# S5 stage of a hybrid decoder trunk: rounding of the frames' turns and the cosines on ScalarE, order and width of GpSimd's projection work

## What is computed

```python
lam = lax.complex(jnp.minimum(a_re, LAMBDA_RE_MAX), a_im)
dt = jnp.exp(log_dt)[:, None]
lam_bar = jnp.exp(lam * dt)
b_bar = ((lam_bar - 1.0) / lam)[:, :, None] * lax.complex(b_re, b_im)
bu = lax.complex(einsum('blgc,gpc->blgp', ug, real(b_bar)), einsum('blgc,gpc->blgp', ug, imag(b_bar)))
_, states = lax.associative_scan(combine, (a, bu), axis=1)   # s[t] = lam_bar*s[t-1] + bu[t]
y = einsum('blgp,gcp->blgc', real(states), c_re) - einsum('blgp,gcp->blgc', imag(states), c_im)
...
return val * jax.nn.sigmoid(gate)     # z = gelu(y + d*u) @ w_glu + b_glu
```

## Time and profile before

| what | value |
|---|---|
| median of 3 runs | 1022.61 us (1021.65 to 1023.76) |
| profiled execution, its own time | 1020.7 us |
| its span | 1018.9 us |
| TensorE busy | 997.9 us, 98% of the span |
| VectorE busy | 820.6 us, 81% |
| ScalarE busy | 487.2 us, 48% |
| GpSimd busy | 274.5 us, 27% |
| granted TensorE clock, mean | 0.994 of full speed |
| chain that ended last, by engine | PE 83%, DVE 10%, issue 3%, ACT 2%, POOL 1% |

### The profile page before, as it was taken

The page is one execution under the profiler, slowest core; times in us unless marked ns, Lnnn a source line. Parts: engine busy times, 40 slices in busy tenths (PEclk is TensorE's granted clock), DMA queues, the critical chain, the costliest instruction groups (busy, mean ns, idle before and its releaser), DMA issues.

```text
span 1018.9 us, 16672 instructions
## 1 busy us (share of the span) xinstructions
PE 997.9 (98%) x5858; PEld 822.7 (81%) x5858; DVE 820.6 (81%) x1154; ACT 487.2 (48%) x883; POOL 274.5 (27%) x231
## 2 busy tenths in 40 slices
PE   9799999999999999999999999999999999999997
PEld 4687888888888888888887776888888888888886
DVE  7994588798898988986895776889898898989844
ACT  7773323444355444543422878655354354543421
POOL 8995887300000000030967240010000000001151
PEclk9899999999999999999999999999999999999998
DMA  6124334122412233230333110232322412224012
GB/s 256 35 47 131 141 107 142 64 84 90 159 62 103 103 118 109 82 124 1 104 128 119 49 42 21 87 123 102 104 84 82 151 76 103 84 102 163 22 42 83
DMA packets 31877, 97.53 MB, mean 96 GB/s; under 512 B 10696, under 2 KB 13256, under 8 KB 27984
## 3 DMA queue, kind: packets, MB, share of 16 engines
q1 hardware_dynamic: 31824, 96.83, 27.3%
HBM read 92.36 MB, written 2.10 MB: 93 GB/s over the span
## 4 chain that ended last, share of the span: by engine, by line
PE 83%; DVE 10%; issue 3%; ACT 2%; POOL 1%; DVEq 0%; ACTq 0%; POOLq 0%
PE ps L1792 17%; PE ps L1795 9%; PE ps L1813 8%; PE ps L1814 8%; PE ps L1815 8%; PE ps L1752 6%; PE ps L1753 6%; PE ps L1754 6%; PE ps L1695 2%; PE ps L1697 2%; PE ps L1696 2%; DVE act L1103 2%; PE ps L1998 1%; PE ps L1973 1%; PE ps L1985 1%
## 5 line engine op out<-in xcount | busy, mean ns | idle before, releaser
L459 POOL TENSOR_TENSOR gate_sb<-gate_sb 128x1 f32<-128x1 f32 x50 | 18.1, 362 | 713.7 <-DMA raw<-panels_in 500.3
L1814 PE MATMUL ps<-hid,w_hi 128*128 128x512 f32 x384 | 150.5, 392 | 0.0
L1813 PE MATMUL ps<-hid,w_hi 128*128 128x512 f32 x384 | 150.4, 392 | 0.0
L1815 PE MATMUL ps<-hid,w_lo 128*128 128x512 f32 x384 | 149.6, 390 | 0.0
L725 ACT ACTIVATE s_hi<-w_raw 128x1024 fp32r<-128x1024 f32 (+1 forms) x104 | 87.8, 844 | 100.4 <-PE ps L1795 94.7
L549 POOL TENSOR_TENSOR w_lo<-raw,w_hi 128x1024 fp32r<-128x1024 f32 x52 | 130.2, 2505 | 4.2
L1792 PE MATMUL ps<-hid,s_hi 128*128 128x512 f32 x448 | 121.3, 392 | 0.5 <-ACT acc L789 0.5
L1752 PE MATMUL ps<-hid,w_hi 128*128 128x512 f32 x304 | 120.3, 396 | 0.0
L1753 PE MATMUL ps<-hid,w_hi 128*128 128x512 f32 x304 | 118.6, 390 | 0.0
L1754 PE MATMUL ps<-hid,w_lo 128*128 128x512 f32 x304 | 118.5, 390 | 0.0
L1213 DVE TENSOR_TENSOR s_lo<-w_raw,s_hi 128x1024 fp32r<-128x1024 f32 (+1 forms) x104 | 101.7, 989 | 17.6 <-ACT s_hi L725 9.9
(11 more groups left out here) (288 smaller groups left out, 2047.5 us busy)
## 6 DMA issues: line engine op xcount, KB each, us to landing
raw<-panels_in SPq DMA_DIRECT2D x108, 512.0 KB, 3.3
w_raw<-pairs_in SPq DMA_DIRECT2D x28, 1024.0 KB, 5.5
xy<-xu_in SPq DMA_DIRECT2D x4, 512.0 KB, 8.2
out<-h SPq DMA_DIRECT2D x8, 256.0 KB, 2.2
prm<-prm_in SPq DMA_DIRECT2D x1, 1280.0 KB, 6.4
h<-x_rows_in SPq DMA_DIRECT2D x1, 1280.0 KB, 13.7
h<-x_rows_in SPq DMA_DIRECT2D x1, 768.0 KB, 5.7
dd<-dd_in SPq DMA_DIRECT2D x1, 256.0 KB, 6.3
```

Of the source, the lines that this page charges most:

```text
L1813: mm(to, w_hi[:, s, w], hid[:, 0, 0, HK * par + k, :], start=(k == 0), stop=False)
L1814: mm(to, w_hi[:, s, w], hid[:, 0, 1, HK * par + k, :], start=False, stop=False)
L1815: last = mm(to, w_lo[:, s, w], hid[:, 0, 0, HK * par + k, :], start=False, stop=(k == HK - 1))
```

## The change

Four edits, all in the S5 stage.

1. ScalarE rounds the turns. A new `frame_round(c)` on ScalarE copies the turns from PSUM to `phases[c]` with ROUND added; VectorE's `frame(c)` becomes one instruction, (phases - ROUND) - turns, the negative fraction. ScalarE's sine gets the scale -2 pi, and the cosine is made as sin(pi/2 - 2 pi |fraction|), in two operations (Abs, Sin with a bias column `quarter`) where there were three.
2. The order on VectorE and ScalarE: VectorE's frame 0 stands before the mean square; ScalarE's roundings are put between its other pieces.
3. `prm` comes in two DMAs, the B part (b_re, b_im, g) first; ScalarE's copies and GpSimd's `c_sum` wait for the C part.
4. GpSimd's `project_im` makes `k_im` for two octets in one instruction, `inputs` scales octet 0, then two at a time, then octet 7; the three weight products of octet 0 stand ahead of the first `project_im`, and the scaling of octet 0 between the weight products of octet 1.

```diff
@@ sync
-            sp.dma_start(prm[:], prm_d).then_inc(s_prm, 16)
+            sp.dma_start(prm[:, B_PRM:], prm_d[:, B_PRM:]).then_inc(s_prm, 16)
+            sp.dma_start(prm[:, 0:B_PRM], prm_d[:, 0:B_PRM]).then_inc(s_prm_c, 16)
@@ gpsimd
             def project_im(o):
-                wait(pool, p_done, 2 * o - 2)
-                tt(k_im[:, o % 2], octet(PR("b_re"), o)...,
-                   x_dif[:, pairs_of(o), :]..., mul).then_inc(k_part, 1)
+                wait(pool, p_done, 2 * o)
+                two = slice(o * OGP, (o + 2) * OGP)
+                tt(k_im.rearrange("p q g j c -> p (q g) j c"), PR("b_re")...[:, two]...,
+                   x_dif[:, two, :]..., mul).then_inc(k_part, 2)
-            def inputs(o):
-                part = xy[:, o * OCT:(o + 1) * OCT, :]
+            def inputs(o, n):
+                part = xy[:, o * OCT:(o + n) * OCT, :]
...
+            pool.wait_ge(s_prm_c, 16)
             tt(c_sum[:], PR("c_re"), PR("c_im"), add).then_inc(setup_p, 1)
             wait(pool, setup_v, SETUP_L)
             pool.wait_ge(setup_p, 4)
-            weights_mul(0, (0,))
+            weights_mul(0)
             wait(pool, setup_v, SETUP_X)
             project_im(0)
-            project_im(1)
-            weights_mul(0, (1, 2))
             weights_sum(0)
-            wait(pool, setup_a, SETUP_RSTD)
-            inputs(0)
             wait(pool, s_dd, 16)
             tt(dd[:, 0], dd[:, 0], dd[:, 1], mul).then_inc(setup_p, 1)
-            weights_mul(1)
+            weights_mul(1, (0,))
+            wait(pool, setup_a, SETUP_RSTD)
+            inputs(0, 1)
+            weights_mul(1, (1, 2))
             weights_sum(1)
-            inputs(1)
+            inputs(1, 2)
...
+            for o in range(2, NO):
+                if o % 2 == 0:
+                    project_im(o)
                 weights_mul(o)
                 weights_sum(o)
-                inputs(o)
+                if o % 2 == 1:
+                    inputs(o, min(2, NO - o))
@@ scalar
-                act_fn(sink_[:, pairs], phase, ACT.Sin, scale=TWO_PI).then_inc(frame_a, 1)
-                act_fn(cosk[:, pairs], phase, ACT.Sin, scale=PI_).then_inc(frame_a, 1)
-                a.wait_ge(frame_a, 4 * c + 2)
-                act_fn(cosk[:, pairs], cosk[:, pairs], ACT.Square).then_inc(frame_a, 1)
-                a.wait_ge(frame_a, 4 * c + 3)
-                act_fn(cosk[:, pairs], cosk[:, pairs], ACT.Copy, scale=-2.0, bias=1.0).then_inc(frame_a, 1)
+                act_fn(sink_[:, pairs], phase, ACT.Sin, scale=-TWO_PI).then_inc(frame_a, 1)
+                act_fn(cosk[:, pairs], phase, ACT.Abs).then_inc(frame_a, 1)
+                a.wait_ge(frame_a, 3 * c + 2)
+                act_fn(cosk[:, pairs], cosk[:, pairs], ACT.Sin, scale=-TWO_PI, bias=quarter[:, 0:1]).then_inc(frame_a, 1)
+
+            def frame_round(c):
+                wait(a, frame_mm, c + 1)
+                act_fn(phases[c], ps[:, frame_bank(c), :], ACT.Copy, bias=ROUND).then_inc(frame_r, 1)
@@ vector
             def frame(c):
-                turned = ps[:, frame_bank(c), :]
-                v.wait_ge(frame_mm, c + 1)
-                wait(v, frame_v, 2 * c)
-                ts(rstd[:], turned, ROUND, ROUND, add, sub).then_inc(frame_v, 1)
-                v.wait_ge(frame_v, 2 * c + 1)
-                tt(phases[c], turned, rstd[:], sub).then_inc(frame_v, 1)
+                v.wait_ge(frame_r, c + 1)
+                stt(phases[c], phases[c], ROUND, ps[:, frame_bank(c), :], sub, sub).then_inc(frame_v, 2)
```

More of the change, by code:

```diff
@@ L94 @@
 N_PRM = _at
+B_PRM = PRM["b_re"][0]
 NPOW = J + 1
@@ L178, in build @@
         eps = sb("eps", [P, 1])
+        quarter = sb("quarter", [P, 1])
         minus = sb("minus", [P, P], F32R)
@@ L253, in build @@
         over.close()
-        s_turns = sem("turns_in")
+        s_turns, s_prm_c = sem("turns_in"), sem("prm_c_in")
+        frame_r, quarter_set = sem("frame_r"), sem("quarter_set")
         s_lam, s_prm, s_cst, s_h, s_col, s_mask, s_dd = (sem(n) for n in (
@@ L480, in project_im @@
             def project_im(o):
-                wait(pool, p_done, 2 * o - 2)
-                tt(k_im[:, o % 2], octet(PR("b_re"), o).unsqueeze(2).to_broadcast([P, OGP, J, C]),
-                   x_dif[:, pairs_of(o), :].unsqueeze(3).to_broadcast([P, OGP, J, C]), mul).then_inc(k_part, 1)
-            def inputs(o):
-                part = xy[:, o * OCT:(o + 1) * OCT, :]
-                tt(part, part, rstd_u[:, 0].unsqueeze(1).to_broadcast([P, OCT, NK]), mul).then_inc(u_done, 1)
+                wait(pool, p_done, 2 * o)
+                two = slice(o * OGP, (o + 2) * OGP)
+                tt(k_im.rearrange("p q g j c -> p (q g) j c"),
+                   PR("b_re").rearrange("p (g c) -> p g c", c=C)[:, two].unsqueeze(2).to_broadcast([P, 2 * OGP, J, C]),
+                   x_dif[:, two, :].unsqueeze(3).to_broadcast([P, 2 * OGP, J, C]), mul).then_inc(k_part, 2)
+            def inputs(o, n):
+                part = xy[:, o * OCT:(o + n) * OCT, :]
+                tt(part, part, rstd_u[:, 0].unsqueeze(1).to_broadcast([P, n * OCT, NK]), mul).then_inc(u_done, n)
             nc.gpsimd.memset(p_0[:], 0.0).then_inc(zeroed, 1)
@@ L600, in _ @@
             act_fn(turn_t[:], ps[0:8, 3, :], ACT.Copy).then_inc(turn_copied, 1)
-            wait(a, s_prm, 16)
+            wait(a, s_prm_c, 16)
             for o in range(NO):
@@ L613, in frame @@
                 wait(a, frame_v, 2 * c + 2)
+                if c == 0:
+                    a.wait_ge(quarter_set, 1)
                 pairs = slice(8 * c, 8 * c + 8)
                 phase = phases[c].rearrange("p (g k) -> p g k", k=NK)
-                act_fn(sink_[:, pairs], phase, ACT.Sin, scale=TWO_PI).then_inc(frame_a, 1)
-                act_fn(cosk[:, pairs], phase, ACT.Sin, scale=PI_).then_inc(frame_a, 1)
-                a.wait_ge(frame_a, 4 * c + 2)
-                act_fn(cosk[:, pairs], cosk[:, pairs], ACT.Square).then_inc(frame_a, 1)
-                a.wait_ge(frame_a, 4 * c + 3)
-                act_fn(cosk[:, pairs], cosk[:, pairs], ACT.Copy, scale=-2.0, bias=1.0).then_inc(frame_a, 1)
+                act_fn(sink_[:, pairs], phase, ACT.Sin, scale=-TWO_PI).then_inc(frame_a, 1)
[5 more added lines that the diff above has]
+                act_fn(phases[c], ps[:, frame_bank(c), :], ACT.Copy, bias=ROUND).then_inc(frame_r, 1)
             def copy_p(o):
@@ L659, in y_to_lo @@
                 act_fn(hid[:, 0, 1, o, :], ps[:, 7, :], ACT.Copy).then_inc(y_lo, 1)
+            frame_round(0)
             copy_p(0)
@@ L664, in _ @@
             evacuate_v(0)
+            frame_round(1)
             frame(0)
@@ L667, in _ @@
             copy_p(1)
+            frame_round(2)
             evacuate_v(1)
+            frame_round(3)
             frame(1)
@@ L926, in _ @@
             nc.vector.memset(eps[:], EPS).then_inc(bank_free, 4)
+            nc.vector.memset(quarter[:], PI_ / 2).then_inc(quarter_set, 1)
             nc.vector.memset(rcol[:], 0.0).then_inc(joined, 4)
@@ L1037, in run_states @@
                 turn = rs.rearrange("p r g k -> p r (g k)")
-                wait(v, frame_a, 4 * (o // 2) + 4)
+                wait(v, frame_a, 3 * (o // 2) + 3)
                 wait(v, st_done, 2 * o)
@@ L1067, in _ @@
             project_sum(0)
+            frame(0)
             mean_square()
-            frame(0)
             project_mul(1)
```

## The result

| what | before | after |
|---|---|---|
| median, 4 runs each on one chip | 1022.77 us (1021.65 to 1023.76) | 1031.52 us (1030.46 to 1032.37) |
| profiled execution, its span | 1018.9 us | 1029.3 us |
| mean granted TensorE clock | 0.994 | 0.993 |

The ratio is 1.009, with an interval of 1.0075 to 1.0105. The change makes the kernel **slower by 0.9%**, some 9 us, outside the range given. The clock is no part of it.

What follows compares the result with a forecast made beforehand. VectorE was taken to bound the run from 18.60 to about 76.5 us, TensorE after. About 3 us of VectorE work saved, less later `k_im` and cosines, left 0.6 us gained: 1022.0 us against 1022.61, range 1020.3 to 1023.4.

Steps and rivals of the forecast that it cites:

- The remaining edits I cost at nothing: GpSimd's later pairs, the extra load on SP's queue and the new constant's memset were taken to add no time.
- The new constant's memset is on an engine that is idle then.: Setting the new constant was taken to cost nothing, as its engine has no work at that time.
- a drain: Rival: the table load before frame 0 costs 1.38 us more on the path, giving 1023.4 us; chance 3%.
- TensorE's clock there: Rival: longer idle before S5's Toeplitz blocks keeps TensorE at the low clock, 2.1 us lost, 1024.7 us; chance 5%.
- `k_im` ready at 17.95: GpSimd's 128x1024 product, behind three weight products, starts at 15.96 and takes 2.0 us; the mean square then ends at 21.75.
- First sine at 24.86, cosines at 26.68, VectorE waiting 1.85: ScalarE's frame 0, behind table load and frame_round(1), makes VectorE wait 1.85 us; scan 0 starts at 26.7, 0.96 later.
- Projection 2 at 33.3: On VectorE, scan 0's 5.30 us and two fused operations of 1.3 put projection 2 at 33.3 against 33.88: 0.6 gained.
- So the start of projection 2 there is the meter: what it moves, the S5 stage moves: Nothing on VectorE changes behind 33.88, so any shift of projection 2's start was taken to shift the S5 stage equally.
- the sign of being wrong that the text itself named: If TensorE doesn't wait for VectorE at fold 7, TensorE is the bound and the forecast is wrong.
- Its spare time, put at 0.8 us: TensorE's 1.09 us wait for VectorE at fold 7 shrinks to about 0.8, as ScalarE's copy_p(2) comes 0.3 late.
- the 0.6 still fits: The 0.6 us gained on VectorE was taken to stay within TensorE's remaining spare time of about 0.8 us.
- The forecast of no measurable change: 1022.0 us against a median of 1022.61, a difference under 0.2%; chance 72%, or 0.86 for any result within 0.2%.

Runs made afterwards that it cites:

- run 1: The changed kernel with its new constant in unused padding, so every tile keeps its address from before: 1021.07 us against 1021.61 for the kernel before, ratio 0.9995.
- run 2: The kernel before with one unused 32-byte tile where the change puts its constant, no instruction different: 1031.83 us, ratio 1.0105.
- run 6: The kernel before with 32 bytes ahead of `w_hi`, so weights and `hid` move together and keep their distance: 1021.46 us, ratio 1.0002.
- run 7: The kernel before with only `w_hi`, `w_lo`, `col`, `acc` and `rstd` 32 bytes further, `hid` in its place: 1031.62 us, ratio 1.0099.
- run 3: The kernel before with an unused 64-byte tile behind `eps`, in front of `hid`: 1024.7 us, ratio 1.0039.
- run 8: The kernel before with an unused 128-byte tile behind `eps`, in front of `hid`: 1030.36 us, ratio 1.0088.
- run 10: The kernel before with an unused 256-byte tile behind `eps`, in front of `hid`: 1021.57 us, ratio 0.9999.
- run 11: The kernel before with an unused 512-byte tile behind `eps`, in front of `hid`: 1021.53 us, ratio 1.0.
- run 9: The kernel of run 1 with GpSimd's first `k_im` product ahead of octet 0's second and third weight products: 1022.28 us, ratio 1.0006 to the kernel before.
- run 12: The kernel before with only `w_lo`, `col`, `acc` and `rstd` 32 bytes further, `w_hi` and `hid` in their places: 1031.76 us, ratio 1.009.
- run 5: The kernel before with 32 bytes behind `hid` only, moving `act`, the split sums and their raw blocks: 1022.47 us against 1021.17, ratio 1.0007.

## Why the prediction was wrong

The step that failed is the last of the sum: "The remaining edits I cost at nothing", and in it "The new constant's memset is on an engine that is idle then." The instruction is indeed free. Its *operand* was not: the column's 32 bytes moved `hid` and `act` from a multiple of 256 bytes behind the weights to 32 past one, which costs 11.2 us in matmuls hundreds of microseconds away. Runs 1 and 2 settle this from both sides (the change without the bytes, the bytes without the change), runs 6 and 7 show that the distance counts, runs 3, 8, 10 and 11 that it counts within 256 bytes. No rival had it. The two that were clearly slower than before put the time into S5, by a drain and by TensorE's clock there; the granted clock over the run is the same (0.993 against 0.994), and the S5 stage isn't where the time went.

The rest, point by point, as far as the profile after and run 1 show it:

- `k_im` ready at 17.95: the half for octet 0 came at 17.70 (15.76 plus 1.93, GpSimd's row above), and the mean square's end at 21.51 instead of 21.75. Right; a 128x1024 product of this form has 1.93 us, for which I took 2.0.
- First sine at 24.86, cosines at 26.68, VectorE waiting 1.85: they were 24.48, 26.38 (25.66 plus 0.72) and 1.70. Right. The operation with the bias column is 0.09 longer than I priced it; the earlier start makes up for it.
- Projection 2 at 33.3: it was 32.91. Scan 0 started at 26.42 instead of 26.7, its 5.30 us held, and the two fused operations took 1.19 instead of 1.3. VectorE gained 0.97 us instead of 0.6.
- "So the start of projection 2 there is the meter: what it moves, the S5 stage moves" failed. That fold 7 doesn't wait for VectorE is the sign of being wrong that the text itself named: TensorE is the bound. Its spare time, put at 0.8 us ("the 0.6 still fits"), was gone: it stood idle 2.34 us at 67.36 for Toeplitz transfers, where the kernel before had no idle above 0.25 us between 53.09 and fold 7 (that one, at 69.96, the text overlooked). The 0.5 us that the profile after is ahead at the end of the stage come near the 0.6 forecast by luck; in run 1's profile the same stage ends 1.2 us late. Run 9 moved the meter by another 1.0 us for nothing.
- The drain behind a table load, the rival that rested on the Trainium skill (ScalarE: Activation LUTs, What ACT_TABLE_LOAD costs): the sine starts 0.02 us behind the end of the load (23.18 plus 1.28, then 24.48). The load's 1.28 us agree with that page; a drain of 1.38 is in no row here.
- The forecast of no measurable change is what the change gives without its bytes: run 1, 0.9995 [0.9985, 1.0005], whose 0.5 us can't be told from none. That agrees in the number; the way there, VectorE's gain passed on by TensorE, doesn't hold. So no version tried beats the kernel before.

What stays open is *how* the distance acts. Work of other engines at the same time isn't it: in the longest stretch of triples without another matmul between them (390, from about 99 us on), the distance of starts from the ninth matmul on is 226.7 ns on average before, and after it is 233 to 235 ns whichever of VectorE, ScalarE and GpSimd are busy around it, 233.4 in the eight cases where none is. (DMA wasn't separated.) That the next weights are read while the matmul streams is in the rows of run 12, and the slowest member there is the one under which the moved tile is read; that two reads get in each other's way is argued from this, not shown, and the slow first member speaks against its simplest form. The Trainium skill (TensorE: Matmul & The Clock Gate, Step-by-step: what each phase is for) says that TensorE has two independent read ports on SBUF and that loading the next tile's weights takes no bandwidth from the running matmul. That statement alone leaves the distance no way to matter; the runs with and without it differ by 10 us, so here the measurement decides, whatever the path is.

## What to carry to other kernels

A tile costs more than its bytes: each one declared moves all that are declared behind it, in stages that the edit doesn't touch. Where a change adds, removes or resizes a tile, list the addresses of both kernels, and where matmuls are the bound, look at the distance between the streamed and the stationary tile modulo 256 bytes; put a small constant into padding, as run 1 did. (Behind the last of the matmuls' tiles should do as well; no run tried it.) When a loss lies where nothing was edited, look at the distance of starts of the same instructions at the same clock, and then at what their operands have that changed.

## What the runs showed of the hardware

- The pace of back-to-back matmuls of 128x512 (fp32r, declared `F32R` in the kernel, each with its own weight load, granted clock 1.00) depends on the distance of the two operands in a partition. Over the whole of the stretch of 390, its head included, they start 227.0 ns apart on average in the kernel before and at 256 and 512 bytes more (runs 10, 11), 233.6 at 32 bytes either way (runs 2, 7), 229.2 at 64 and 232.6 at 128 (runs 3, 8). Other distances weren't run. The weight loads themselves have 187 to 189 ns in all of these kernels.
- Even at the good distance the first few matmuls of a unit go at the slow pace (0.232 in run 6), and then the fast one sets in. In the unit shown they come behind four half-width matmuls, 113 to 120 ns apart; whether that is the reason wasn't tried.
- Half-width matmuls (256 columns) don't lose by it: those that stream `hid` against `w_hi` and `w_lo` have a median of 120 ns before and 118 after, so "misplaced is slower" is no rule for every width.
- The matmuls with `s_hi` and `s_lo` take 273.8 us before and 273.5 after, but there all their operands move together. In run 5, where `hid` stays and they move, they take 274.9.
- The S5 stage scatters more than it could gain: run 1's runs lie between 1019.7 and 1023.6 us, and in one execution or the other TensorE does the sums of octet 2 at the lower clock level (1.97 us, the kernel before) or at the higher (1.15, run 5, with the same S5 program).
